# Three GLA stages of a two-block transformer kernel that read their split weights in other patterns

## The reference

```python
def gla_mixer(h, w_in, w_a2, b_a, g_norm, w_out):     # h: 256 x 2048
    proj = h @ w_in                                   # 2048 x 6160
    q, k, v, r, a_lr = jnp.split(proj, [GLA_DK, 2 * GLA_DK, 2 * GLA_DK + GLA_DV, 2 * GLA_DK + 2 * GLA_DV], axis=-1)
    ...
    o = rms_norm_2(o, g_norm).reshape(B, S, GLA_DV) * jax.nn.silu(r.astype(f32))
    return o.astype(h.dtype) @ w_out                  # 2048 x 2048
```

## Time and profile before

| | |
|---|---|
| median of two runs | 2705.29 us |
| span of the profiled execution | 2703.8 us |
| TensorE busy in the span | 97% |
| VectorE, ScalarE, GpSimd busy | 66%, 48%, 8% |
| granted TensorE clock, mean | 0.998 |
| DMA engines, mean GB/s | 217 |
| L468 to L470, one product of 512 columns | 389 to 397 ns from start to end |
| L1010, one split on ACT | 1060 ns |
| L1581, one split on DVE | 1234 ns |

### The profile page before, as it was taken

How to read it: one execution, slowest core, us unless ns; L and a number is a source line. 1 busy time by engine, 2 the same in 40 slices (tenths; PEclk the granted TensorE clock), 3 DMA queues, 4 the chain that set the end, 5 groups by cost and what they waited for, 6 DMA issues and landing times.

```text
span 2703.8 us, 34387 instructions
## 1 busy us (share of the span) xinstructions
PE 2634.7 (97%) x12073; PEld 2168.5 (80%) x12073; DVE 1790.2 (66%) x2052; ACT 1293.1 (48%) x1563; POOL 222.6 (8%) x162
## 2 busy tenths in 40 slices
PE   1999999999999999999999999999999999999999
PEld 0788888888888888888888887877888888888887
DVE  6977776878778666666666855577555555555555
ACT  1445554445455444444444564556554444444443
POOL 0000000100000000000000310131001111111110
PEclk9999999999999999999999999999999999999999
DMA  9978777677886666666666556643666666666664
GB/s 372 380 266 299 268 256 232 228 252 261 312 278 221 204 202 203 204 204 203 203 202 190 189 166 186 180 142 127 197 187 189 191 189 191 188 192 189 191 191 135
DMA packets 280498, 585.49 MB, mean 217 GB/s; under 512 B 21761, under 2 KB 24221, under 8 KB 279509
## 3 DMA queue, kind: packets, MB, share of 16 engines
q1 hardware_dynamic: 280404, 584.26, 66.8%
HBM read 582.01 MB, written 2.11 MB: 216 GB/s over the span
## 4 chain that ended last, share of the span: by engine, by line
PE 94%; DVE 3%; DMA 2%; issue 1%; ACT 0%; SPq 0%; DVEq 0%; ACTq 0%
PE lin L468 29%; PE lin L470 29%; PE lin L469 29%; DMA sb_ada<-in_w_ada_dram 2%; DVE sb_acc L1680 1%; PE aux L770 1%; PE aux L502 1%; DVE sb_wlo L1581 1%; PE aux L781 0%; PE aux L954 0%; PE aux L468 0%; PE aux L470 0%; PE aux L469 0%; PE aux L525 0%; DVE sb_gm L2322 0%
## 5 line engine op out<-in xcount | busy, mean ns | idle before, releaser
L1581 DVE TENSOR_TENSOR sb_wlo<-sb_raw,sb_whi 128x1024 fp32r<-128x1024 f32 x896 | 1102.3, 1234 | 802.5 <-ACT sb_whi L1010 799.4
L1010 ACT ACTIVATE sb_whi<-sb_raw 128x1024 fp32r<-128x1024 f32 x896 | 947.9, 1060 | 1237.6 <-PE lin L470 1141.1
L468 PE MATMUL lin<-sb_whi,sb_act_hi 128*128 128x512 f32 x2720 | 1078.8, 397 | 2.0 <-DVE sb_wlo L1581 1.5
L470 PE MATMUL lin<-sb_whi,sb_act_lo 128*128 128x512 f32 x2720 | 1060.5, 390 | 0.0
L469 PE MATMUL lin<-sb_wlo,sb_act_hi 128*128 128x512 f32 x2720 | 1059.0, 389 | 0.0
L468 PEld LDWEIGHTS lin<-sb_whi,sb_act_hi 128*128 128x128 f32 x2720 | 510.9, 188 | 111.3 <-issue 9.6
L470 PEld LDWEIGHTS lin<-sb_whi,sb_act_lo 128*128 128x128 f32 x2720 | 510.5, 188 | 108.2
L469 PEld LDWEIGHTS lin<-sb_wlo,sb_act_hi 128*128 128x128 f32 x2720 | 511.3, 188 | 104.2 <-issue 2.6
L468 PE MATMUL lin<-sb_whi,sb_hid_hi 128*128 128x512 f32 x704 | 275.3, 391 | 0.0
L470 PE MATMUL lin<-sb_whi,sb_hid_lo 128*128 128x512 f32 x704 | 274.1, 389 | 0.0
L469 PE MATMUL lin<-sb_wlo,sb_hid_hi 128*128 128x512 f32 x704 | 273.9, 389 | 0.0
(11 more groups left out here) (351 smaller groups left out, 1664.7 us busy)
## 6 DMA issues: line engine op xcount, KB each, us to landing
sb_raw<-in_w_in_dram SPq DMA_DIRECT2D x176, 512.0 KB, 6.5
sb_raw<-in_ffn_w_gu_dram SPq DMA_DIRECT2D x176, 512.0 KB, 3.7
sb_ada_in<-in_w_ada_dram SPq DMA_DIRECT2D x128, 512.0 KB, 4.2
sb_raw<-in_gla_w_in_dram SPq DMA_DIRECT2D x96, 512.0 KB, 3.8
sb_raw<-in_w_gate_dram SPq DMA_DIRECT2D x88, 512.0 KB, 3.8
sb_raw<-in_w_up_dram SPq DMA_DIRECT2D x88, 512.0 KB, 4.4
sb_raw<-in_w_down_dram SPq DMA_DIRECT2D x88, 512.0 KB, 5.6
sb_raw<-in_ffn_w_down_dram SPq DMA_DIRECT2D x88, 512.0 KB, 3.6
```

Of the source, the lines that this page charges most:

```text
L468: pe.matmul(o, h, whi[:, w], start=first and q == 0, stop=False)
L470: m = pe.matmul(o, l, whi[:, w], start=False, stop=last and q == 1)
L1010: act.activation(whi[:, idx % RING * HALF:(idx % RING + 1) * HALF], raw[:, idx // 2 % RING, idx % 2 * HALF:(idx % 2 + 1) * HALF], ACT.Copy ...
L1581: dve.tensor_tensor(wlo[:, c], raw[:, idx // 2 % RING, idx % 2 * HALF:(idx % 2 + 1) * HALF], whi[:, c].bitcast(fp32), ALU.subtract).then_i ...
```

## The change

In GQ and GV the split weights are laid out in another order in `whi` and `wlo`, and read in the matching pattern; what is computed does not change. Within a k-tile of 512 columns, column b * (512 / B) + a is stored at place a * B + b, with B = 2 in GQ and 16 in GV (`STRANDS`). ACT and DVE read `raw` in order and write (DVE also reads `whi`) with a step of B places: 8 bytes in GQ, 64 bytes in GV. TensorE reads the weights with the same step, B runs of 512 / B columns, so that the columns reach PSUM in their old order; PSUM is written without gaps. The stationary operands, the number of products, and all waits are as before.

In GO the weights lie as before, and each product of 512 columns becomes two of 256: three products on the first 256 columns of a bank, then three on the other 256, each with its own load of the stationary operand. `start` clears the bank once.

```diff
+STRANDS = {"GQ": 2, "GV": 16}
+def strands(phase, it, per, idx):
+    if not isinstance(it, int):
+        return None
+    half = H0[phase] + it * per + idx
+    return next((b for name, b in STRANDS.items() if 0 <= half - H0[name] < 32), None)
...
+    strand_of = lambda t, b: t.rearrange("p (k a b) -> p k b a", k=2, b=b)
+    columns_of = lambda t, b: t.rearrange("p (k b a) -> p k b a", k=2, b=b)
...
-                w = slice(idx % RING * HALF + q * NB, idx % RING * HALF + (q + 1) * NB)
+                w, w_hi, w_lo = slice(idx % RING * HALF, (idx % RING + 1) * HALF), whi[:], wlo[:]
                 o, t = (banks or lin[gi % 2])[tb][:], slice(tb * P, (tb + 1) * P)
                 h, l = (part(x, kt + q)[:, t] for x in (x_hi, x_lo))
-                pe.matmul(o, h, whi[:, w], start=first and q == 0, stop=False)
-                pe.matmul(o, h, wlo[:, w], start=False, stop=False)
-                m = pe.matmul(o, l, whi[:, w], start=False, stop=last and q == 1)
+                if phase == "GO":
+                    for n in range(2):
+                        w = slice(idx % RING * HALF + q * NB + n * NB // 2, idx % RING * HALF + q * NB + (n + 1) * NB // 2)
+                        c, once = o[:, n * NB // 2:(n + 1) * NB // 2], dict(skip_group_check=True)
+                        pe.matmul(c, h, whi[:, w], start=first and q == 0 and n == 0, stop=False, **once)
+                        pe.matmul(c, h, wlo[:, w], start=False, stop=False, **once)
+                        m = pe.matmul(c, l, whi[:, w], start=False, stop=last and q == 1, **once)
+                    continue
+                if phase in STRANDS:
+                    b = STRANDS[phase]
+                    w_hi, w_lo = strand_of(whi[:, w], b)[:, q], strand_of(wlo[:, w], b)[:, q]
+                    o, w = o.rearrange("p (b a) -> p b a", b=b), slice(0, b)
+                else:
+                    w = slice(idx % RING * HALF + q * NB, idx % RING * HALF + (q + 1) * NB)
+                pe.matmul(o, h, w_hi[:, w], start=first and q == 0, stop=False)
+                pe.matmul(o, h, w_lo[:, w], start=False, stop=False)
+                m = pe.matmul(o, l, w_hi[:, w], start=False, stop=last and q == 1)
...
+            b = strands(phase, it, per, idx)
+            if b:
+                high, new = strand_of(high, b), columns_of(new, b)
+            act.activation(high, new, ACT.Copy).then_inc(hi_made, 1)
...
+            if b:
+                low, new, high = strand_of(low, b), columns_of(new, b), strand_of(high, b)
+            dve.tensor_tensor(low, new, high, ALU.subtract).then_inc(lo_made, 1)
```

More of the change, by code:

```diff
@@ L1009, in split @@
                 act.wait_ge(half_used, H0[phase] + it * per + idx - RING + 1)
-            act.activation(whi[:, idx % RING * HALF:(idx % RING + 1) * HALF],
-                           raw[:, idx // 2 % RING, idx % 2 * HALF:(idx % 2 + 1) * HALF], ACT.Copy).then_inc(hi_made, 1)
+            high, new = whi[:, idx % RING * HALF:(idx % RING + 1) * HALF], raw[:, idx // 2 % RING, idx % 2 * HALF:(idx % 2 + 1) * HALF]
+            b = strands(phase, it, per, idx)
+            if b:
+                high, new = strand_of(high, b), columns_of(new, b)
+            act.activation(high, new, ACT.Copy).then_inc(hi_made, 1)
         def body(it, phase, per, hooks, upto=None, start=RING):
@@ L1580, in split @@
             c = slice(idx % RING * HALF, (idx % RING + 1) * HALF)
-            dve.tensor_tensor(wlo[:, c], raw[:, idx // 2 % RING, idx % 2 * HALF:(idx % 2 + 1) * HALF],
-                              whi[:, c].bitcast(fp32), ALU.subtract).then_inc(lo_made, 1)
+            low, new, high = wlo[:, c], raw[:, idx // 2 % RING, idx % 2 * HALF:(idx % 2 + 1) * HALF], whi[:, c].bitcast(fp32)
+            b = strands(phase, it, per, idx)
+            if b:
+                low, new, high = strand_of(low, b), columns_of(new, b), strand_of(high, b)
+            dve.tensor_tensor(low, new, high, ALU.subtract).then_inc(lo_made, 1)
         def ada_add(n, kt=None, half=None):
```

## The result

The changed kernel takes 2872.95 us (median of two runs, 2872.86 and 2873.05) against 2705.29: 1.062 times as long, with a 95% interval from 1.060 to 1.064, or +167.7 us. The clock stayed at 0.998. The first rows of the page answer: TensorE's busy time and the chain have grown, and the two splits have grown a little. VectorE has dropped from 66% to 63% of a longer span.

The account below looks back on a forecast made before the run. The prediction took TensorE, busy for 97% of the span, to bound the kernel. Profiled span 2703.8 plus 1.5 to the median, plus 0 (GQ), 81.9 (GV) and 2.8 (GO) gave 2790 us, range 2704 to 2884.

Parts of the forecast that it names:

- the likeliest case: Whole kernel: GQ free, GV at about half rate, GO slightly longer; 2790 us, from 2783 to 2798, chance 0.45.
- the second rival: TensorE's reads in GQ and GV: every step halves the stream, two apart as well; 2872 to 2882 us, chance 0.15.
- the free case: Whole kernel: TensorE reads any step at full rate, so time stays within 2%; 2706 to 2720 us, chance 0.24.
- GO's +2.8: Products of 256 columns in GO: 768 at 117 ns each in place of 87.1 us, +2.8 us.
- GQ's 0 in the sum: TensorE's reads two columns apart in GQ cost nothing: 0 us, with bounds 0 and +82.
- GV, +81.9: TensorE's reads sixteen columns apart in GV go at half rate, 440 ns for 226.7 a product: +81.9 us.
- something other than the array holds the fast stream back: TensorE's fast stream: 6% over its cycles was taken to mean it is near the limit of its reads.
- the first rival: TensorE reads any step at full rate; 6% may be a fixed 5 ns per product; 2706 to 2720 us, chance 0.24.
- the rival with 216 ns: Stationary loads in GO hide behind nothing: 216 ns a product, +79 us in place of +2.8, 2866 us, chance 0.06.
- The conversions: Splits in GV on ScalarE and VectorE slow to 1.94 and 2.32 us, hidden under a GV of 179 us.
- if TensorE is not slowed ... some waits of TensorE for L1581 appear, a few us: In GV with TensorE at full rate, VectorE is at 95% of 96.8 us and TensorE waits a few us.
- Quarter rate: TensorE's reads: two apart at half rate in GQ, sixteen apart at a quarter in GV; about 3056 us, chance 0.10.
- Not slower: TensorE reads any step at full rate, GV's step staying at 226.7 ns; 2706 to 2720 us, chance 0.24.

Follow-up runs that it names:

- the last kernel: Against the kernel before the change, split weights of every stage stored and read in runs of four columns, starts 16 apart: 2687.72 us against 2705.33, ratio 0.9935.
- the first experiment: Against the kernel before the change, only TensorE's weight reads changed: runs of two columns in GQ, GV, GR, of four in GO: 2954.78 us beside 2705.16.

## Why the prediction was right and wrong

The measured 2872.95 us lies inside the range (2704 to 2884) and outside the likeliest case's own (2783 to 2798). It is the second rival that happened, "every step halves the stream, two apart as well", whose 2872 to 2882 holds it and which had 0.15. The range held by luck in this sense: it was wide enough to take in a rival thought unlikely, while the likeliest sum, 2790, missed by 83 us. Two small slips of its sums change nothing: the likeliest case ends at 2797, not 2798, and the free case with GO's +2.8 begins at 2708, not 2706.

**The failed step is GQ's 0 in the sum.** Its bounds were 0 and +82; the term came to 384 x (451 - 227) = +86, the stage to +85.5. The choice within the bounds went by "the nearest stepped rows are those of the other engines, and they are free". The rows of those engines were read rightly (at runs of one element L2326 even reads both of its inputs with that step, not one): in GQ the splits took 1.12 and 1.23 us at the median, against 1.06 and 1.23, inside the 92 ns allowed. What doesn't carry over is the rate. From the prediction's own figures ScalarE takes an element each 0.86 ns and VectorE each 1.06, so two to a line give them a line's time of 1.7 and 2.1 ns. TensorE takes a column each 0.417 ns and needs four from a line to give it 1.67. That all three engines meet the same limit of some 1.7 ns to a line fits these rows, but wasn't tested as such, and TensorE's single columns, at 0.82 to 0.93 ns a line, don't fit it.

The Trainium skill ("Advanced Engine Details and Errata", section "SBUF Cachelines"), on which the prediction drew, says that at least two accesses must fall on a line. The splits of GQ, 1.12 and 1.23 us with two on a line, agree with it. For TensorE's fp32r operand the measurement differs and decides: two on a line run at half rate (451 ns for 227), four are needed.

**GV, +81.9, was right in kind and near in size.** The step was 434 ns for 440, the term 384 x 207 = 79.5, the stage +78.8. The reason given was weak: "something other than the array holds the fast stream back" read 6% over the cycles as nearness to a limit of reading. The steps at 256 and 512 columns show 13 ns a product and one cycle a column, as the first rival had offered with another size (5 ns). The step does lie at a limit, since 384 columns from 128 lines are no faster than 512, but the 6% didn't show that. The ranking of the two patterns was wrong too: two apart was priced below sixteen apart and is the dearer by 17 ns.

**GO, +2.8, was small as said.** 120 ns for 117: 768 x 120 - 87.1 = +5.1, the stage +4.1. The 117 came from products with loads of 16 columns. The loads of 128 stay hidden (111 ns back to back), so the rival with 216 ns falls.

**The conversions** in GV took 1.95 us on both engines, for 1.94 and 2.32: VectorE's price per element, taken twice, was too high. That hid behind TensorE, as forecast. The step "if TensorE is not slowed ... some waits of TensorE for L1581 appear, a few us" fell in the run with the change's writes alone: no microsecond, with VectorE at 83% and not 95%.

**Quarter rate** (0.10, left out of the range) fell: sixteen apart is no slower than two apart. **Not slower** fell with it, at the place it named, a step of 434 in GV.

## What to carry to other kernels

A row of one engine with a stepped operand says little of another until both are put as elements per nanosecond: a pattern that is free for an engine taking an element in 0.9 to 1.1 ns halved one that takes one in 0.417. Keep TensorE's moving fp32r operand in runs of at least four aligned columns (16 bytes), in any order within them, and the runs near one another: starts 8 or 16 columns apart cost 233 and 224 ns for 227, starts 64 apart 278. At 16 apart the layout can be permuted in the whole kernel, and the engines that write it pay nothing (1059 and 1235 ns a split). Price a change on a saturated TensorE by the step between products in its stage, not by busy shares: those were 100% in GQ before and after.

## What the runs showed that wasn't expected

- A line that gives one column costs half of what a line giving two to four costs, 0.82 to 0.93 against 1.63 to 1.75 ns (lines up to 16 columns apart). So one read and two reads per line come out alike per column, and a step of sixteen is no worse than a step of two. Why isn't known; no run looks inside it.
- Whole lines far apart cost up to 51 ns a product (278 ns at 64 columns) and lines 16 columns apart gain 2 to 3. With 16 apart the steps lie between 217 and 239 ns and repeat in a fixed order: every 24 products, two halves, in the last kernel, but in GO of the first experiment every seven between 2172 and 2185 us (the 239 ns falls on each of the three products by turns) and every four between 2190 and 2208 us (230, 224, 221, 218). Seven fits no order of the operands, which come in threes and in halves of 12, so their addresses alone don't set the step; what does stays open.
- ScalarE and VectorE take the same 1.95 us for a split at sixteen apart, though they differ in order (1.06 and 1.23): 1.9 ns an element, the line's time again.
